# Expert results added by the scatter DMA onto a copy of h, instead of stored by rank and summed on VectorE

## What is computed

```python
h = h + mix
h = h + grouped_moe(rms_norm(h, norm_ffn[i]), w_router, w_gate_e[i], w_up_e[i], w_down_e[i])
ple_gate = jax.nn.sigmoid(rms_norm(h, norm_ple[i]) @ w_ple_gate[i])
h = h + ple_gate * (p[i] @ w_ple_proj[i])
...
# grouped_moe: 16 experts; each token has exactly two of them, with weights that sum to 1
for e in range(N_EXPERTS):
    hidden = jax.nn.silu(xt @ w_gate[e]) * (xt @ w_up[e])
    y = y + combine[:, e:e + 1] * (hidden @ w_down[e])
```

## Time and profile before

| | |
|---|---|
| median of 3 runs | 1453.73 us (1446.99 to 1455.87) |
| the profiled execution | 1455.25 us, span 1453.5 us |
| mean granted TensorE clock | 0.899 of full speed |
| busy: TensorE, VectorE, ScalarE, GpSimd | 89%, 61%, 50%, 10% |
| DMA: hardware queue, software queue | 240.41 MB, 40.15 MB |

### The profile page before, as it was taken

One profiled execution on the slowest core, in us unless ns is written; L12 is line 12 of the kernel. 1 busy time (PEld: TensorE's weight loads), 2 busy tenths in 40 slices (PEclk: granted clock), 3 DMA queues, 4 the chain that ended last, 5 costly groups with the idle time before them and its releaser, 6 DMA issues.

```text
span 1453.5 us, 17201 instructions
## 1 busy us (share of the span) xinstructions
PE 1291.3 (89%) x6016; PEld 1045.4 (72%) x6016; DVE 893.5 (61%) x1031; ACT 731.5 (50%) x837; POOL 143.7 (10%) x105
## 2 busy tenths in 40 slices
PE   4989998977999999996979899998689999999793
PEld 3778886866887787773858767777678777877472
DVE  3733357354888888884651344333488888888553
ACT  4533202123777777774342343413277777777532
POOL 0000000000112222211000000000012221121100
PEclk9999999976999999998979855588699999999897
DMA  7312111423999998996312200023289999989501
GB/s 309 116 59 99 47 58 59 145 102 104 342 349 337 350 351 334 348 365 241 105 60 93 71 1 0 15 74 129 73 291 348 341 355 347 361 342 352 195 15 58
DMA packets 48597, 281.28 MB, mean 194 GB/s; under 512 B 9392, under 2 KB 9392, under 8 KB 19232
## 3 DMA queue, kind: packets, MB, share of 16 engines
q1 hardware_dynamic: 33408, 240.41, 44.6%
q0 software_dynamic: 15136, 40.15, 7.6%
HBM read 274.23 MB, written 23.07 MB: 205 GB/s over the span
## 4 chain that ended last, share of the span: by engine, by line
PE 56%; DMA 18%; DVE 10%; issue 7%; ACT 4%; POOL 2%; DVEq 1%; POOLq 0%; SPq 0%; ACTq 0%
PE psum L336 51%; DMA yscr<-arena,cur 16%; DVE wlo L1288 3%; ACT whi L895 2%; PE psum L397 2%; PE psum L820 2%; DVE alo L1598 2%; POOL arena L1858 1%; DVE arena L1317 1%; DMA arena<-yscr 1%; DMA raw<-w_dense_dram 1%; PE psum L592 1%; DVE arena L1606 1%; ACT arena L934 1%; DMA arena<-vscr,cur 1%
## 5 line engine op out<-in xcount | busy, mean ns | idle before, releaser
L1288 DVE TENSOR_TENSOR wlo<-raw,whi 128x2048 fp32r<-128x2048 f32 x227 | 515.6, 2289 | 189.5 <-ACT whi L895 183.2
L895 ACT ACTIVATE whi<-raw 128x2048 fp32r<-128x2048 f32 x227 | 433.7, 1914 | 201.7 <-PE psum L336 192.0
L336 PE MATMUL psum<-whi,ahi 128*128 128x512 f32 (+1 forms) x1184 | 479.5, 405 | 45.6 <-DVE wlo L1288 26.7
L336 PE MATMUL psum<-whi,alo 128*128 128x512 f32 (+1 forms) x1184 | 466.9, 394 | 0.0
L336 PE MATMUL psum<-wlo,ahi 128*128 128x512 f32 (+1 forms) x1184 | 466.6, 394 | 0.0
L336 PEld LDWEIGHTS psum<-whi,ahi 128*128 128x128 f32 x1184 | 228.6, 193 | 103.3 <-issue 28.9
L336 PEld LDWEIGHTS psum<-whi,alo 128*128 128x128 f32 x1184 | 227.6, 192 | 49.1
L336 PEld LDWEIGHTS psum<-wlo,ahi 128*128 128x128 f32 x1184 | 228.8, 193 | 43.5
L336 PE MATMUL psum<-arena 128*128 (+8 forms) x1060 | 208.5, 374 | 5.5 <-ACT arena L1090 3.1
L336 PEld LDWEIGHTS psum<-arena 128*128 128x128 f32 (+3 forms) x1060 | 160.9, 231 | 59.0 <-issue 42.3
L895 ACT ACTIVATE ahi<-psum 128x512 fp32r<-128x512 f32 x140 | 79.2, 593 | 135.0 <-PE psum L592 78.9
(11 more groups left out here) (157 smaller groups left out, 850.3 us busy)
## 6 DMA issues: line engine op xcount, KB each, us to landing
raw<-w_moe_dram SPq DMA_DIRECT2D x192, 1024.0 KB, 9.0
raw<-w_dense_dram SPq DMA_DIRECT2D x35, 1024.0 KB, 6.9
arena<-yscr POOLq DMA_DIRECT2D x8, 1024.0 KB, 6.1
vscr<-arena POOLq DMA_DIRECT2D x8, 512.0 KB, 2.9
arena<-gains_dram POOLq DMA_DIRECT2D x7, 512.0 KB, 3.8
h<-x_dram SPq DMA_DIRECT2D x4, 512.0 KB, 9.4
arena<-w_proj_dram POOLq DMA_DIRECT2D x2, 1024.0 KB, 6.4
out_dram<-arena POOLq DMA_DIRECT2D x4, 512.0 KB, 2.9
```

The lines of the kernel that those rows point to most:

```text
L336: return nc.tensor.matmul(o, l, r, start=start, stop=stop, **kw)
L895: return nc.scalar.activation(o, i, ACT.Copy, scale=scale)
L1288: tt(wlo[:, b % SPL, :], raw[:, b % RAW, :], halves(whi[:, b % SPL, :]), ALU.subtract).then_inc(lo_ready, 1)
```

## The change

The two half-results of a token no longer go to rows of their own. Per layer there is a DRAM tensor `hscr` of 512 rows. After the mixer's output has been added, GpSimd stores the four tiles of h there, behind the stores of `vscr` and ahead of the gain's load. Each scatter then adds its rows to those of `hscr` in the DMA (`compute_op=ALU.add`), at the row of the token, with the scatters one after another as before. At the end SP waits for the last scatter and loads the four tiles back over h, each with its own semaphore; `square` waits for that. GpSimd's loads of `yscr`, VectorE's sums and two small operations on the target rows in the router are gone; `target` takes the token's number in place of the target row.

```diff
@@ SP
+            def reload(layer):
+
+                sp.wait_ge(M[layer]["sca"], 16 * EXP)
+                for tb in range(TB):
+                    sp.dma_start(h[:, tb, :], hscr[layer][tb * P:(tb + 1) * P, :])\
+                      .then_inc(s_x[tb], 16)
...
                 for c in range(B + MOE_CHUNKS, B + MOE_CHUNKS + last):
+                    if c == B + MOE_CHUNKS + 4:
+                        reload(layer)
                     load(c, w_dense[d])
                     d += 1
+            reload(1)
@@ ScalarE, square
+                elif n in (2, 5):
+                    act.wait_ge(s_x[tb], 16 * (n // 3) + 32)
                 else:
-                    act.wait_ge(h_ready, (n - 1) * TB + tb + 1)
+                    act.wait_ge(h_ready, SUMS[n] * TB + tb + 1)
@@ VectorE, router and target
-                link(ts(v["a"], v["rank"], float(SEQ), -FAR, ALU.mult, ALU.add))
-                link(tt(info[:, :, :, 1], v["a"], tk, ALU.add))
...
-                    ts(cur[:, 2:3], v["idx"][:, bass.ds(e * 4 + 1, 1)], FAR, None, ALU.add)\
+                    ts(cur[:, 2:3], v["idx"][:, bass.ds(e * 4, 1)], FAR, None, ALU.add)\
                         .then_inc(m["cw"], 1)
@@ VectorE, ple
-                def add_experts(tb):
-
-                    dve.wait_ge(s_y[tb % 2], 16 * (tb // 2 + 1) + 32 * layer)
-                    y = area(AR_YC + tb % 2 * CW, 2, D)
-                    link(tt(h[:, tb, :], h[:, tb, :], y[:, 0, :], ALU.add))
-                    tt(h[:, tb, :], h[:, tb, :], y[:, 1, :], ALU.add).then_inc(h_ready, 1)
@@ GpSimd
+                for tb in range(TB):
+                    pool.wait_ge(h_ready, SUMS[n] * TB + tb + 1)
+                    pool.dma_start(hscr[layer][tb * P:(tb + 1) * P, :], h[:, tb, :])\
+                        .then_inc(s_hw, 16)
                 gain(n + 1)
...
                 def scatter(e):
+                    if isinstance(e, int) and e == 0:
+                        pool.wait_ge(s_hw, 16 * TB * (layer + 1))
                     ready((m["ou"], 2 * e + 2),
                           (m["cw"], 2 * e + 2))
                     nc.gpsimd.indirect_dma_start(
-                        out=yscr[layer],
+                        out=hscr[layer],
                         out_offset=bass.IndirectOffsetOnAxis(ap=cur[:, 2:3], axis=0),
                         in_=area(AR_OUT, D), in_offset=None,
-                        bounds_check=last_target, oob_is_err=False).then_inc(m["sca"], 16)
+                        bounds_check=last_row, oob_is_err=False,
+                        compute_op=ALU.add).then_inc(m["sca"], 16)
...
-                for tb in range(TB):
-                    if tb >= 2:
-                        pool.wait_ge(h_ready, (n * TB) + tb - 1)
-                    pool.dma_start(area(AR_YC + tb % 2 * CW, 2, D),
-                                   yscr[layer].rearrange("(k t) d -> t k d", k=2)
-                                   [tb * P:(tb + 1) * P, :, :])\
-                        .then_inc(s_y[tb % 2], 16)
```

More of the change, by code:

```diff
@@ L106, in build @@
 def build(nc, consts, hconsts, aconsts, gains, lbl, bout, x, pT, w_dense, w_moe, w_proj, out,
-          vscr, yscr):
+          vscr, hscr):
     f32, f32r, i32 = mybir.dt.float32, mybir.dt.float32r, mybir.dt.int32
@@ L184, in build @@
         s_rows = sems("s_rows", TB)
-        s_y = sems("s_y", 2)
+        s_hw = sem("s_hw")
         p_ready = sem("p_ready")
@@ L238, in build @@
         FFN = {1: 0, 4: 1}
+        SUMS = {1: 0, 3: 1, 4: 2, 6: 3}
         ORDER = {0: 0, 2: 1, 3: 2, 5: 3}
@@ L326, in _ @@
                     sp.wait_ge(f["pe"], 5 * STEPS)
+                    sp.wait_ge(f["sca"], 16 * STEPS)
                 last = (ATT - PLE0 + 9) if layer == 0 else 4
                 for c in range(B + MOE_CHUNKS, B + MOE_CHUNKS + last):
+                    if c == B + MOE_CHUNKS + 4:
+                        reload(layer)
                     load(c, w_dense[d])
                     d += 1
+            reload(1)
         @block.tensor
@@ L639, in moe @@
                 x_T(0, 0, 0)
-                pe.wait_ge(h_ready, 3 * layer * TB + TB)
+                pe.wait_ge(h_ready, 2 * layer * TB + TB)
                 def step(e, b, e6, nxt, prev=True, nx2=True):
@@ L1172, in ple @@
                         elif g >= 6:
-                            act.wait_ge(h_ready, n * TB + g - 5)
+                            act.wait_ge(h_ready, SUMS[n + 1] * TB + g - 5)
                         elif g == 0:
@@ L1203, in _ @@
                         act.wait_ge(s_acon, 16)
-                        act.wait_ge(h_ready, 3 * TB)
+                        act.wait_ge(h_ready, 2 * TB)
                     nc.scalar.activation(QT[:, i * 4 + q, :], PS[q][:, :], ACT.Identity,
@@ L1660, in ple @@
                 k = BLK["ple0"] if layer == 0 else BLK["ple1"]
-                def add_experts(tb):
-                    dve.wait_ge(s_y[tb % 2], 16 * (tb // 2 + 1) + 32 * layer)
-                    y = area(AR_YC + tb % 2 * CW, 2, D)
-                    link(tt(h[:, tb, :], h[:, tb, :], y[:, 0, :], ALU.add))
-                    tt(h[:, tb, :], h[:, tb, :], y[:, 1, :], ALU.add).then_inc(h_ready, 1)
-                add_experts(0)
                 for tb in range(TB):
-                    if tb + 1 < TB:
-                        add_experts(tb + 1)
                     norm_x(n, tb)
@@ L1713, in further @@
                         for i in range(2):
-                            ts(cur[:, i:i + 1], PS[7][:, i:i + 1], FAR, None, ALU.add)\
+                            ts(cur[:, i:i + 1], PS[7][:, 0:1], FAR, None, ALU.add)\
                                 .then_inc(f["dve"], 1)
@@ L1816, in gain @@
                 pool.dma_start(area(AR_GAIN, D), gains[n]).then_inc(s_gain, 16)
-            last_row, last_target = pool.to_reg(SEQ - 1), pool.to_reg(2 * SEQ - 1)
+            last_row = pool.to_reg(SEQ - 1)
             gain(0)
@@ L1896, in _ @@
                             nc.gpsimd.indirect_dma_start(
-                                out=yscr[layer],
+                                out=hscr[layer],
                                 out_offset=bass.IndirectOffsetOnAxis(ap=cur[:, 1:2], axis=0),
                                 in_=area(AR_OUT, D), in_offset=None,
-                                bounds_check=last_target, oob_is_err=False)\
-                                .then_inc(f["sca"], 16)
+                                bounds_check=last_row, oob_is_err=False,
+                                compute_op=ALU.add).then_inc(f["sca"], 16)
                     pool.wait_ge(f["sca"], 16 * STEPS)
-                for tb in range(TB):
-                    if tb >= 2:
-                        pool.wait_ge(h_ready, (n * TB) + tb - 1)
-                    pool.dma_start(area(AR_YC + tb % 2 * CW, 2, D),
-                                   yscr[layer].rearrange("(k t) d -> t k d", k=2)
-                                   [tb * P:(tb + 1) * P, :, :])\
-                        .then_inc(s_y[tb % 2], 16)
                 gain(n + 2)
                 if layer == 0:
-                    pool.wait_ge(h_ready, 2 * TB)
+                    pool.wait_ge(m["ou"], 2 * EXP)
                     pool.dma_start(ar[:, AR_AC:AR_AC + ACONST_N], aconsts).then_inc(s_acon, 16)
@@ L2008 @@
     aps["vscr"] = [nc.dram_tensor(f"vscr{j}", (SEQ, D), f32).ap() for j in range(LAYERS)]
-    aps["yscr"] = [nc.dram_tensor(f"yscr{j}", (2 * SEQ, D), f32).ap() for j in range(LAYERS)]
+    aps["hscr"] = [nc.dram_tensor(f"hscr{j}", (SEQ, D), f32).ap() for j in range(LAYERS)]
     build(nc, **aps)
```

## The result

The changed kernel takes 1469.09 us (median of 4 runs, 1468.15 to 1474.05), the one before 1454.8 (4 runs here, one more than above). The ratio is 1.0124, with a 95% interval of 1.0085 to 1.0163: slower by 14 us where the sum had 56 (-9.6 + 66). The direction and the place were right, the size was not. The profiled execution has a span of 1467.8 us, 14.3 above the old 1453.5, so it stands for the difference well.

A forecast was written before the change was run, and what follows sets the result against it. The prediction took the expert loop through the scatter's landing as the bound, with TensorE nearly so. From 1455.25 us, -9.6 for the layer ends and +66 for the add gave 1511.7 us (+4.0%), range 1445 to 1600.

The forecast's parts named there:

- Which loop bounds the expert stage: Expert loop: scatter landing, target, index, gather, next scatter set the 19.36 us period; TensorE, 97% busy, is nearly the bound.
- The layer's end: Reading h back without VectorE's sums: gains 7.4 us in layer 0 and 2.2 in layer 1, together -9.6.
- about 3 us are covered: Layer's end: if the last scatter lands later, TensorE's four free PSUM banks hide about 3 us.
- The layer's start: Four stores of h ahead of the gain load: no cost, 9 us of cover before the first gather.
- SP's queue: The reload stands ahead of nine attention chunks needed only tens of us later: no cost.
- the router: Two small operations fewer, ahead of a wait for TensorE's ranks: nothing counted.
- The add, 2.2 us for each scatter: Expert loop: the accumulate lengthens each scatter's landing by 2.2 us, times 30 scatters: +66 us.
- A longer one costs its whole length: Expert loop: any lengthening costs in full, since no link idles by more than 0.3 us.
- the free add: Rival for the scatters: the add lengthens no landing (delta 0), time 1445.7 us; chance 0.12.
- The rivals: Other outcomes, mostly by the add's length per scatter from 0 to 9.1 us; the forecast itself had chance 0.38.
- engine time alone: Rival for the scatters: the add costs 0.7 us each, 21 in all, time 1466.7 us; chance 0.14.
- The page's rule: Scatters: a reducing transfer moves at half speed, so the moving phase doubles, the 2.2 or 3.5 us case.

The follow-up runs named there:

- e5: Kernel before, with target indices, weights and result area doubled (even and odd experts), so VectorE and ScalarE wait for scatter e-2, order kept: 1434.25 us, ratio 0.985.
- e6: Changed kernel, add kept, with target indices, weights and result area doubled for even and odd experts: 1423.11 us, ratio 0.9782.
- e11: Changed kernel with only the first half of each weight chunk loaded in the expert loop: 1421.5 us, one run.
- e10: Kernel before with only the first half of each weight chunk loaded in the expert loop: 1432.22 us, one run.
- e9: Kernel before with two extra VectorE sums (2.4 us) per step in the expert loop, no add in the DMA: 1503.8 us, ratio 1.0385.
- e2: Kernel before with one extra VectorE sum (1.2 us) per step in the expert loop, no add in the DMA: 1469.78 us, ratio 1.0126.
- e1: Changed kernel with the add taken out of the scatter, rows written over hscr: 1441.44 us against 1453.75 for the kernel before, ratio 0.9921.
- e8: Kernel before with SP's weight loads in the expert loop released one split later, one chunk fewer on its way: 1454.25 us, ratio 1.0011.
- e3: Kernel before with GpSimd's scatter issued ahead of the gather in each step: 1534.03 us, ratio 1.0572.
- e4: Changed kernel with GpSimd's scatter issued ahead of the gather in each step: 1615.17 us, ratio 1.112.
- e7: Changed kernel with one extra VectorE sum of 1.2 us per step in the expert loop: 1501.58 us.

## Why the prediction was wrong in size

- **Which loop bounds the expert stage**: right. Scatter, target, index, gather, scatter. e5 and e6 cut it and TensorE's own period appeared, 18.65 us. The granted clock stayed at 1.00 in the loop, as the sum had it, but TensorE fell to 94% busy and not to 87%.
- **The layer's end**: forecast -9.6 in all, -7.4 and -2.2; the profile has -6.2 and -1.0. The first square does follow the copies (687.76, right behind 687.27). The last of the copies starts 13.8 us behind the scatter's issue instead of 13.3, for the longer landing: of its 2.8 us my "about 3 us are covered" covered 2.3. Then 16.9 us to the last copies into ahi instead of my 16.0.
- **The layer's start, SP's queue, the router**: nothing seen; the first gather is issued at 331.87, 0.7 sooner.
- **The add, 2.2 us for each scatter**: right as a price of the transfer. 2.0 in e11 against e10, 1.8 to 2.0 in the loop against e9 at the same period, and at the layer's end 2.2 for the moving alone (2.8 with the descriptors, which the term left out).
- **The failed step is "A longer one costs its whole length"**, from which the sum took 30 x 2.2. I looked for idle time in the loop and found none, and took the 11 us of a landing for a fixed length. It is mostly the price of sharing with the weights: 3.2 us alone, 5.8 beside half of them. And it gets shorter when the loop gets longer: e2 took back four fifths of 1.2 us, e9 about three fifths of 2.4, most of it in the transfers. The term was 30 x 0.92 = 27.7 instead of 30 x 2.2 = 66. My account is that the weights are released by VectorE's splits, which the same loop holds back, so that a longer loop has a thinner stream beside its transfers; this part is argued (below). I had both rows, 3.18 and 11.5, and used them to argue against the free add alone.
- Smaller: the sum missed the shorter drain (1.9), and the rest of the change gains 12.3 rather than 9.6: 7.2 of it at the layers' ends, the rest in e1's shorter loop of layer 0.
- **The rivals**: the measured time, 1469.1, lies at the "engine time alone" case, 1466.7, but not by its mechanism: the add's price is not 0.7 us, it is about 2 us, and more than half of it is given back. That the time lies inside the range is luck. No rival had the landing shrink with a longer loop.
- **The page's rule** that a reduce needs two source reads on one ring and so moves at half the speed ("Collectives: The Full Stack" of the Trainium skill, section "The bandwidth ceiling: the fold count and why AG ≠ RS ≠ AR"; there for a collective's ring): the time agrees where the scatter is alone, 4.4 us of moving for 2.2. The engine time doubles only beside the full stream (9.9 engine-us more on 11.4); alone it is 2.6 times as much (28.0% of 5.97 us for 20.1% of 3.18, so 26.7 for 10.2 engine-us). A second read is seen in no trace.

What stays open is why the transfers get shorter. That the stream of weights is thinner just when they run is argued from e2, e9, e10 and the order of releases; no run moved the loads against the gather by themselves (e8 was meant to and did not). The packets of the traces bear it out in part only. Over a gather's whole flight the hardware queue's share of the engines is the same 0.78 before, in e2 and in e9, and 0.82 in the changed kernel (means of layer 0). Only behind the gather's first packet, some 5 us after its issue, are the weights slower: 253 GB/s before, 201 in e2, 196 in e9, 229 in the changed kernel. And e1 has the sooner gathers of layer 0 with a shorter loop and more bytes, 357 GB/s for 346, so the length of the loop is not all.

## What to carry to other kernels

A transfer's landing, when it shares the engines with a stream that the same loop paces, was not a constant of this loop: before multiplying an extra cost by the number of steps, look at how long the same transfer takes alone, and lengthen the loop by plain work of that size, to see how much of it comes back. A cost inside a tight loop is worth asking first whether the loop must be there: here one more result area and one more column of indices were worth 19 us before the change and 46 after it, and made the change a gain. And before one transfer is issued ahead of another on a queue, look at how much earlier than needed the second lands; here it was 2 to 3 us, and turning them round cost 80.

## What the runs showed of the hardware that was not expected

GpSimd's last drain, at the very end of the program, is 8.15 us long in every profile with plain scatters (before, e1, e2, e3, e5, e8, e9, e10) and 6.23 in every one with adding scatters (after, e4, e6, e7, e11). Kernel before, then changed kernel:

```profile
L112 POOLq DRAIN  x1: 8152/8152/8152, 1445.1 to 1445.1; - x1
```

```profile
L112 POOLq DRAIN  x1: 6233/6233/6233, 1461.4 to 1461.4; - x1
```

The split follows the add in the scatters and not hscr, the layer's end or the weights (e1 has hscr and no add, and drains for 8.15). It is worth 1.9 us of the end, and its cause is open.
